# Two-stack sequence model on one core: the branch products of layers 1 and 2 as split products

## The chip, the cores and the metric

The kernel runs on one core of a Trainium2 chip. The time is that of the device for one execution, in microseconds (us). TensorE (PE in the profile) multiplies, VectorE (DVE), ScalarE (ACT) and GpSimd (POOL) work on elements, SyncE (SP) issues the weight loads.

## The reference

256 tokens of width 1024 pass through four layers, two of a first kind (called layers 1 and 2 here, `L` = 0 and 1 in the code) and two of a second. All is float32. A layer of the first kind has four mixers (retention, SSD, gated linear attention, mLSTM), each 256 wide, whose outputs are weighed with gates and merged:

```
    u = h @ w_in
    ...
    y_ret = (head_rmsnorm(o, ret_norm_g).reshape(bsz, seq, MIX_W) * jax.nn.silu(rg)).astype(h.dtype)
    ...
    ybr = jnp.stack([y_ret, y_ssd, y_gla, y_ml], axis=2)
    gates = jax.nn.sigmoid(mgate.reshape(bsz, seq, N_BRANCH, D_MODEL))
    merged = jnp.sum(gates * jnp.einsum('bsnv,nvd->bsnd', ybr, w_branch), axis=2)
    return merged @ w_out
```

The change is about the `einsum` with `w_branch`: four products of 256 tokens x 256 by 256 x 1024 in each of the two layers.

## The kernel before

The 256 tokens are two tiles (`T` = 2) of 128 rows. The branches are taken in the order SSD, mLSTM, retention, gated attention; `b` is 0 to 3 in this order, and "branch 0" to "branch 3" below are these.

**Two kinds of product.** Most products are split: the weights are cut into pieces of 1024 columns. ScalarE rounds a piece to a high part (`w_hi`, written by `high_parts`, line 1859), GpSimd or VectorE subtracts it from the original and has the low part (`w_lo`, lines 844 and 2926), and TensorE makes three matmuls of the rounded type for one exact product (`split_product`, lines 1004 to 1006: high x high, low rows x high weights, high rows x low weights). The four branch products of layers 1 and 2 (`merge` on TensorE, line 1130) are plain float32 matmuls, straight from the loaded weights in `ring`; the hardware runs each as two passes.

**Places.** There are four places for pieces (`NPIECE`). A piece's high part is written when the piece four before it has been used by TensorE. Pieces are made in one order for all engines; `M` is the number of the first piece of a layer behind its first six projections. Before the change M+8 to M+39 are the gates' 32 pieces, whose low parts GpSimd makes (two instructions of 512 columns for a piece), and M+40 on are those of the output product, by VectorE.

**Banks.** Four PSUM banks (`pb`) go round among the jobs listed in `bank_jobs1`. A job may open its bank when the job four before it has been emptied. The last jobs ahead of the gates of branch 2 are the four of product 0 (two halves `h` of 512 columns, two tiles `i`): the gates of branch 2 need the first two of these emptied, by VectorE. The gates of branch 3 need the second and third of product 1.

**The order.** Each engine runs a list written out by hand (the functions `mixers`). On TensorE the scans' small products stand between halves of the gates' jobs (`gate`). For each branch VectorE takes its output `y` from PSUM, norms it (`head_norm`, lines 2344 to 2355, with `rsqrt`, lines 2247 to 2254, for the root) and signals `y_ready`. TensorE turns it (`y_turned`, line 1119), ScalarE copies the turned rows to `yT` (line 1792), and TensorE makes the product (`merge`). VectorE weighs it with the gates and adds it up (`merge`, lines 2377 to 2385). On VectorE the head norm of branch `b + 1` stands ahead of the merge of branch `b`. The weights lie in two slots of `ring`, loaded alternately by SyncE when the slot's last reader is done.

## Time and profile before

| | us |
|---|---|
| median of three runs | 2436.46 (2432.53 to 2437.64) |
| profiled execution, its own time | 2435.75 |
| its span | 2433.9 |
| TensorE busy | 2353.2 (97%) |
| VectorE busy | 1693.3 (70%) |
| ScalarE busy | 1407.6 (58%) |
| GpSimd busy | 427.9 (18%) |
| the 128 plain passes of the branch products, first to last start | 177.9 to 733.1 |

The span is what the profiler sees from the first to the last instruction; the execution's own time is 1.85 us longer. A line number in a row is that of the listing. "x16" is the number of instructions in the row, and "[0.43 <-..]" behind a row is how long the engine stood idle before it and what ended that. Times of starts are from the span's start. A row of the timeline with several instructions gives the time from the first start to the last end.

### The profile page before, as it was taken

How to read it: one execution, taken by the hardware profiler on the slowest of the kernel's cores; microseconds unless marked ns; L12 is line 12 of the kernel's file. 1: busy time of each engine (PE TensorE's matmuls, PEld its weight loads, DVE VectorE, ACT ScalarE, POOL GpSimd, SP SyncE). 2: the span in 40 equal slices, each digit the busy share in tenths (PEclk: the TensorE clock that was granted, in tenths of full speed). 3: DMA queues.
4: the chain of work that ended last, by engine and by line, in shares of the span. 5: the costliest groups of instructions: out<-in, count | busy, mean ns of one | idle time of the engine just before them, and what ended most of it. 6: DMA issues, size and time to landing. Idle time of an engine off the chain costs nothing.

```text
span 2433.9 us, 32355 instructions
## 1 busy us (share of the span) xinstructions
PE 2353.2 (97%) x11899; PEld 1953.9 (80%) x11899; DVE 1693.3 (70%) x2327; ACT 1407.6 (58%) x1779; POOL 427.9 (18%) x381
## 2 busy tenths in 40 slices
PE   7999999899998999999999999899989989998998
PEld 7986788798867888888888888788878878887886
DVE  5847655576576999989889898883475557347555
ACT  4543344455433888888878888645444444645443
POOL 1256000004540000000000000075600007560000
PEclk9999999999998999999999999999999999999999
DMA  6534666244335999999999999844475634447450
GB/s 215 191 121 172 208 209 207 89 165 149 129 139 191 362 344 351 361 341 367 344 344 366 342 360 350 296 140 158 160 258 171 204 115 137 170 163 247 167 196 35
DMA packets 384550, 549.77 MB, mean 226 GB/s; under 512 B 27410, under 2 KB 283784, under 8 KB 384312
## 3 DMA queue, kind: packets, MB, share of 16 engines
q1 hardware_dynamic: 380080, 535.82, 64.9%
q0 software_dynamic: 4080, 11.96, 1.5%
q8 instruction: 69, 1.13, 0.2%
q10 hardware_dynamic: 288, 0.59, 0.1%
q14 instruction: 33, 0.27, 0.0%
HBM read 547.28 MB, written 1.05 MB: 225 GB/s over the span
## 4 chain that ended last, share of the span: by engine, by line
PE 85%; DVE 6%; DMA 4%; POOL 2%; issue 1%; ACT 1%; SPq 0%; ACTq 0%; DVEq 0%; POOLq 0%
PE mb L1004 14%; PE mb L1006 14%; PE mb L1005 14%; PE pb L1004 10%; PE pb L1006 9%; PE pb L1005 9%; DMA ring<-in_w_in 2%; PE pb L1130 2%; DVE w_lo L2926 2%; POOL w_lo L844 1%; PE mb L1396 1%; DMA down_w<-in_moe_w 1%; PE pb L1474 1%; DVE conv L2299 1%; PE mb L1157 1%
## 5 line engine op out<-in xcount | busy, mean ns | idle before, releaser
L2926 DVE TENSOR_TENSOR w_lo<-ring,w_hi 128x1024 fp32r<-128x1024 f32 x464 | 558.7, 1221 | 172.9 <-ACT w_hi L1859 126.3
L844 POOL TENSOR_TENSOR w_lo<-ring,w_hi 128x512 fp32r<-128x512 f32 x304 | 390.6, 1321 | 1324.1 <-DVE xn L2733 797.0
L1859 ACT ACTIVATE w_hi<-ring 128x1024 fp32r<-128x1024 f32 x360 | 371.4, 1055 | 272.5 <-PE pb L1006 163.0
L1004 PE MATMUL mb<-w_hi,hT_hi 128*128 128x512 f32 x1232 | 492.1, 399 | 1.6 <-DVE xg_lo L2926 1.1
L1006 PE MATMUL mb<-w_lo,hT_hi 128*128 128x512 f32 x1232 | 481.2, 391 | 0.0
L1004 PE MATMUL pb<-w_hi,hT_hi 128*128 128x512 f32 (+1 forms) x928 | 349.8, 377 | 5.2 <-POOL w_lo L844 3.2
L2926 DVE TENSOR_TENSOR w_lo<-down_w,w_hi 128x1024 fp32r<-128x1024 f32 x242 | 293.7, 1222 | 84.7 <-ACT w_hi L1859 79.3
L1006 PE MATMUL pb<-w_lo,hT_hi 128*128 128x512 f32 (+1 forms) x928 | 342.2, 369 | 0.0
L1005 PE MATMUL pb<-w_hi,low_rows 128*128 128x512 f32 (+1 forms) x928 | 341.9, 368 | 0.0
L2028 ACT ACTIVATE w_hi<-ring 128x1024 fp32r<-128x1024 f32 x256 | 268.5, 1057 | 30.4 <-PE mb L1006 21.9
L1005 PE MATMUL mb<-w_hi,xg_lo 128*128 128x512 f32 x704 | 274.6, 390 | 0.0
L1004 PEld LDWEIGHTS mb<-w_hi,hT_hi 128*128 128x128 f32 x1232 | 231.6, 188 | 49.8 <-DVE w_lo L2926 3.6
L1006 PEld LDWEIGHTS mb<-w_lo,hT_hi 128*128 128x128 f32 x1232 | 231.5, 188 | 49.6
L1004 PEld LDWEIGHTS pb<-w_hi,hT_hi 128*128 128x128 f32 x928 | 175.8, 189 | 39.4 <-DVE merged L2788 3.8
L1005 PE MATMUL mb<-w_hi,low_rows 128*128 128x512 f32 x528 | 206.0, 390 | 0.0
L2028 ACT ACTIVATE w_hi<-down_w 128x1024 fp32r<-128x1024 f32 x176 | 187.0, 1063 | 31.0 <-PE mb L1006 26.7
L1006 PEld LDWEIGHTS pb<-w_lo,hT_hi 128*128 128x128 f32 x928 | 175.7, 189 | 29.7
L1005 PEld LDWEIGHTS pb<-w_hi,low_rows 128*128 128x128 f32 x928 | 175.9, 190 | 27.1 <-issue 0.3
L2926 DVE TENSOR_TENSOR w_lo<-third_gu,w_hi 128x1024 fp32r<-128x1024 f32 x132 | 159.3, 1221 | 37.4 <-ACT w_hi L1859 30.6
L1005 PEld LDWEIGHTS mb<-w_hi,xg_lo 128*128 128x128 f32 x704 | 132.5, 188 | 24.8
L1004 PE MATMUL mb<-w_hi,fhT_hi 128*128 128x512 f32 x352 | 137.7, 391 | 0.0
L1006 PE MATMUL mb<-w_lo,fhT_hi 128*128 128x512 f32 x352 | 137.3, 390 | 0.0
(515 smaller groups left out, 3592.1 us busy)
## 6 DMA issues: line engine op xcount, KB each, us to landing
ring<-in_moe_w SPq DMA_DIRECT2D x128, 1024.0 KB, 9.5
ring<-in_w_in SPq DMA_DIRECT2D x50, 2048.0 KB, 8.0
down_w<-in_moe_w SPq DMA_DIRECT2D x88, 1024.0 KB, 12.3
third_gu<-in_moe_w SPq DMA_DIRECT2D x48, 1024.0 KB, 11.0
down_w<-in_w_ffn_down SPq DMA_DIRECT2D x22, 1024.0 KB, 10.0
ring<-in_w_out SPq DMA_DIRECT2D x8, 2048.0 KB, 7.9
ring<-in_ffn_w SPq DMA_DIRECT2D x16, 1024.0 KB, 8.0
ring<-in_w_ffn_gate SPq DMA_DIRECT2D x16, 1024.0 KB, 5.4
```

The costliest lines, as they stand in the source:

```text
L844: ins = nc.gpsimd.tensor_tensor(w_lo[:, m % NPIECE, cols], source[m][0][:, cols], w_hi[:, m % NPIECE, cols].bitcast(F32), ALU.subtract)
L1004: mm(o, a_hi, hi, start=start, stop=False)
L1005: mm(o, a_lo, hi, start=False, stop=False)
L1006: return mm(o, a_hi, lo, start=False, stop=stop)
L1130: ins = mm(bank[:], yT[:, b % 2, kk, i * P:(i + 1) * P], w[:, kk, h * 512:(h + 1) * 512], start=kk == 0, stop=kk == 1)
L1157: ins = mm(banks[i][:, h * w:(h + 1) * w], probs[:, h, at:at + P], v(j, h), start=n == 0, stop=n == len(parts) - 1)
L1396: ins = mm(mb[2 + half][:, (k % 4) * P:(k % 4 + 1) * P], xn[:, i, k * P:(k + 1) * P], sel[:, i], start=i == 0, stop=i == T - 1)
L1474: ins = mm(bank[:, 0:n], hT[:, k, i * P:(i + 1) * P], wv[:, k], start=k == 0, stop=k == KD - 1)
L1859: f(w_hi[:, m % NPIECE], src, ACT.Copy).then_inc(w_hi_ready, 1)
L2028: f(w_hi[:, n % NPIECE], expert_piece(c, q), ACT.Copy).then_inc(e_hi_ready, 1)
L2299: ins = stt(out=conv[:, blk, s:S], in0=ch_in[:, blk, 0:S - s], scalar=w(3 - s), in1=conv[:, blk, s:S], op0=ALU.mult, op1=ALU.add)
L2926: return tt(dst, src, hi.bitcast(F32), ALU.subtract)
```

## The change

The branch products of layers 1 and 2 become split products, by the function that layers 3 and 4 already used (`merge2`, now `merge`). Their weights become pieces, two for each branch, that stand between those of the gates: behind M+23 come two of product 0, then eight of gates 2, two of product 1, four of gates 3, two of product 2, four of gates 3, two of product 3; the output product begins at M+48. GpSimd makes their low parts. The turned rows are written as a high part by ScalarE (`turned_high`, to `y_odd_hi`) and a low part by VectorE (`turned_low`, to `y_rows_lo`). Each branch's weights have a slot of `ring` for themselves, in two loads; the slot is free when the low parts are made.

```diff
-    items = [("proj", c) for c in range(len(CHUNKS1))]
-    items += [("gate", b, h) for b in range(NBR) for h in range(2)]
+    items = [("proj", c) for c in range(len(CHUNKS1))] + [("gate", b, h) for b in range(2) for h in range(2)]
+    merge = lambda b: [("merge", b, h) for h in range(2)]
+    items += merge(0) + [("gate", 2, 0), ("gate", 2, 1)] + merge(1) + [("gate", 3, 0)] + merge(2) + [("gate", 3, 1)] + merge(3)
...
-                low_parts(MIX[L] + HEAD_PIECES + 8, MIX[L] + HEAD_PIECES + 40)
+                low_parts(MIX[L] + HEAD_PIECES + 8, MIX[L] + HEAD_PIECES + 48)
...
+            def merge_rows(L, b, hs=range(2)):
+                pe.wait_ge(dve_emptied, BK[L].emptied(("yturn", b))[1])
+                merge(L, b, row_parts, hs)
+
+            def merge(L, b, parts, hs=range(2)):
+
+                n_k = branch_k(L, b)
                 for h in hs:
...
+                    banks = [open_bank(BK[L], ("merge", b, h, i)) for i in range(T)]
+                    for q in range(n_k // 2):
+                        m = PC.of[(L, "merge", b, h, q)]
+                        hi, lo = parts[q]
+                        pe.wait_ge(*low_done(m))
+                        for i in range(T):
+                            it = slice(i * P, (i + 1) * P)
+                            for kk in range(2):
+                                k = 2 * q + kk
+                                ins = split_product(banks[i][:], hi[:, kk, it], lo[:, kk, it], m, slice(kk * 512, (kk + 1) * 512),
+                                                    k == 0, k == n_k - 1)
...
-                high_to(M + 24)
-                yturned(L, 0)
+                row_high = row_parts[0][0]
+                turned_high(L, ("yturn", 0), row_high)
+                high_to(M + 26)
                 gate(L, 1, 1)
-                high_to(M + 28)
+                high_to(M + 30)
                 act.wait_ge(gla_arg, 2 * L + 1)
...
                 v.wait_ge(o_read, 4 * L + 2)
+                turned_low(L, 1, ("yturn", 0), row_parts[0])
                 head_norm(L, 1, 3, u_ml[:, :, ML_O:ML_O + MW], False)
                 merge(L, 0)
...
                 v.wait_ge(o_read, 4 * L + 3)
+                turned_low(L, 2, ("yturn", 1), row_parts[0])
                 head_norm(L, 2, 0, u_ret[:, :, 768:1024], False)
                 merge(L, 1)
...
                 head_norm(L, 3, 2, u_gla[:, :, 4 + MW:], False)
-                low_range(M + 40, M + 42)
-                merge(L, 3)
+                turned_low(L, 4, ("yturn", 3), row_parts[0])
+                merge(L, 3, (0,))
+                low_range(M + 48, M + 50)
+                merge(L, 3, (1,))
```

ScalarE, layer 1, from the copies of retention's turned rows (`conv`) to the first exponents of the gated attention, before:

```order
L1953 ACTIVATE conv<-mb 128x512 x2
L1792 ACTIVATE yT<-pb 128x512
L1792 ACTIVATE gates<-pb 128x512 x2
L1859 ACTIVATE w_hi<-ring 128x1024 x4
L1960 ACT_TABLE_LOAD
```

and now:

```order
L1961 ACTIVATE conv<-mb 128x512 x2
L1896 ACTIVATE y_odd_hi<-pb 128x512
L1865 ACTIVATE w_hi<-ring 128x1024 x2
L1798 ACTIVATE gates<-pb 128x512 x2
L1865 ACTIVATE w_hi<-ring 128x1024 x4
L1969 ACT_TABLE_LOAD
```

Two high parts, those of product 0, now stand behind the turned rows and ahead of the second half of the gates of branch 1.

VectorE, layer 1, at the head norm of branch 1, now (before, the same without the row of `y_rows_lo`):

```order
L2569 TENSOR_TENSOR y<-mb,small 128x256 x2
L2934 TENSOR_TENSOR y_rows_lo<-pb,y_odd_hi 128x512
L2347 TENSOR_TENSOR scratch<-y 128x512
L2349 TENSOR_REDUCE small<-scratch 128x8
L2350 TENSOR_SCALAR small<-small 128x8
L2250 TENSOR_SCALAR small<-small 128x8
L2251 TENSOR_TENSOR small<-small 128x8
```

It goes on with the root's other six small instructions, three of 512 columns on `y`, and the merge of product 0. The turned rows' low part has come ahead of the norm.

VectorE, the end of the mixers of layer 1, before:

```order
L2355 TENSOR_TENSOR y<-y,u_gla 128x512
L2926 TENSOR_TENSOR w_lo<-ring,w_hi 128x1024 x2
L2382 TENSOR_TENSOR gates<-pb,gates 128x512
L2385 TENSOR_TENSOR merged<-merged,gates 128x512
L2382 TENSOR_TENSOR gates<-pb,gates 128x512
```

and now:

```order
L2358 TENSOR_TENSOR y<-y,u_gla 128x512
L2934 TENSOR_TENSOR y_rows_lo<-pb,y_odd_hi 128x512
L2393 TENSOR_TENSOR gates<-pb,gates 128x512
L2396 TENSOR_TENSOR merged<-merged,gates 128x512
L2393 TENSOR_TENSOR gates<-pb,gates 128x512
L2396 TENSOR_TENSOR merged<-merged,gates 128x512
L2934 TENSOR_TENSOR w_lo<-ring,w_hi 128x1024 x2
L2393 TENSOR_TENSOR gates<-pb,gates 128x512
```

The two pieces of the output product have moved from ahead of the merge of product 3 to between its halves. GpSimd has in each of the two layers, in one row each, now

```order
L858 TENSOR_TENSOR w_lo<-ring,w_hi 128x512 x80
```

where 64 of the same kind (line 844) stood.

## Rows read from the trace of the kernel before

**Rows 1.** The page: busy time of TensorE; the chain's shares by engine.
```profile
PE 2353.2 (97%) x11899; PEld 1953.9 (80%) x11899; DVE 1693.3 (70%) x2327; ACT 1407.6 (58%) x1779; POOL 427.9 (18%) x381
...
PE 85%; DVE 6%; DMA 4%; POOL 2%; issue 1%; ACT 1%; SPq 0%; ACTq 0%; DVEq 0%; POOLq 0%
```

**Rows 2.** Timeline of TensorE, layer 1: start, duration, instruction.
```profile
177.24 0.39 PE L1004 MATMUL pb<-w_hi,hT_hi 128*128 128x512 f32 x1
...
177.92 7.03 PE L1130 MATMUL pb<-ring,yT 128*128 128x512 f32 x16
184.88 0.70 PE L1146 MATMUL mb<-conv 64*128 64x256 f32 x4
...
186.39 0.50 PE L1004 MATMUL pb<-w_hi,hT_hi 128*128 128x512 f32 x1
...
219.57 0.50 PE L1004 MATMUL pb<-w_hi,hT_hi 128*128 128x512 f32 x1
```

**Rows 3.** All of line 1130: ns least/median/most, first and last start.
```profile
L1130 PE MATMUL pb<-ring,yT x128: 590/592/697, 177.9 to 733.1; 128*128 128x512 f32 x128
```

**Rows 4.** Timeline of GpSimd, layer 1, and one row of layer 2 (647.83).
```profile
179.74 10.00 POOL L844 TENSOR_TENSOR w_lo<-ring,w_hi 128x512 fp32r<-128x512 f32 x8 [9.68 <-ACT w_hi L1859]
194.98 10.37 POOL L844 TENSOR_TENSOR w_lo<-ring,w_hi 128x512 fp32r<-128x512 f32 x8 [5.24 <-ACT w_hi L1859]
215.25 10.01 POOL L844 TENSOR_TENSOR w_lo<-ring,w_hi 128x512 fp32r<-128x512 f32 x8 [9.90 <-ACT w_hi L1859]
...
647.83 9.96 POOL L844 TENSOR_TENSOR w_lo<-ring,w_hi 128x512 fp32r<-128x512 f32 x8 [9.72 <-ACT w_hi L1859]
```

**Rows 5.** Timeline of ScalarE, layer 1.
```profile
173.16 0.61 ACT L1792 ACTIVATE yT<-pb 128x512 f32<-128x512 f32 x1
176.76 0.60 ACT L1792 ACTIVATE gates<-pb 128x512 f32<-128x512 f32 x1 [2.99 <-PE pb L1006]
...
178.62 3.88 ACT L1859 ACTIVATE w_hi<-ring 128x1024 fp32r<-128x1024 f32 x4
```

**Rows 6.** Timeline of VectorE, layer 1, head norm of branch 1 to merge 0.
```profile
174.55 0.69 DVE L2344 TENSOR_TENSOR scratch<-y 128x512 f32<-128x512 f32 x1
...
179.27 0.69 DVE L2355 TENSOR_TENSOR y<-y,u_ml 128x512 f32<-128x512 f32 x1
180.00 0.69 DVE L2377 TENSOR_TENSOR merged<-pb,gates 128x512 f32<-128x512 f32 x1
```

**Rows 7.** VectorE beside GpSimd: head norm 0 (layer 1), and layer 4.
```profile
149.35 1.66 DVE L2344 TENSOR_TENSOR scratch<-y 128x512 f32<-128x512 f32 x1
...
2047.88 0.16 DVE L2251 SCALAR_TENSOR_TENSOR small<-small 128x2 f32<-128x2 f32 x1
2048.02 5.07 POOL L844 TENSOR_TENSOR w_lo<-ring,w_hi 128x512 fp32r<-128x512 f32 x4 [3.58 <-ACT w_hi L1859]
2048.08 1.26 DVE L2252 TENSOR_TENSOR small<-small 128x2 f32<-128x2 f32 x1
2049.37 1.22 DVE L2253 TENSOR_TENSOR small<-small 128x2 f32<-128x2 f32 x1
```

**Rows 8.** VectorE, layer 1: last exponents; end of head norm 2.
```profile
202.82 1.37 DVE L2404 TENSOR_TENSOR ch_in<-gT 128x128 f32<-128x128 f32 x1
...
213.15 0.69 DVE L2355 TENSOR_TENSOR y<-y,u_ret 128x512 f32<-128x512 f32 x1
```

**Rows 9.** End of the mixers of layer 1: VectorE, and TensorE's next product.
```profile
260.96 0.69 DVE L2382 TENSOR_TENSOR gates<-pb,gates 128x512 f32<-128x512 f32 x1 [5.58 <-PE pb L1130]
...
267.48 1.28 DVE L2926 TENSOR_TENSOR low_rows<-pb,hT_hi 128x512 fp32r<-128x512 f32 x2
...
269.01 0.47 PE L1004 MATMUL pb<-w_hi,hT_hi 128*128 128x512 f32 x1 [0.25 <-DVE low_rows L2926]
```

**Rows 10.** Stretches of 4 us: busy time by engine, granted clock (PEclk), DMA.
```profile
1580.00:1584.00 4.00, 2.74 (x10) 2.10 (x11) 2.33 (x2) 2.50 (x5) 0.00 (x0) 0.50 0.68 250
1584.00:1588.00 4.00, 4.00 (x9) 2.07 (x8) 2.61 (x10) 3.76 (x6) 0.00 (x0) 0.67 0.01 2
```

150 lines of the change are left out of this document (65 added, 85 removed).

## The prediction

> **What bounds the kernel now.** I read the shares of busy time first, then the chain that ended last, then the timeline of each engine in layer 1 from 170 to 270 us. TensorE is busy for 97% of the span and carries 85% of the chain [rows 1]: a stage gets shorter only if TensorE has less to do in it, and longer as soon as TensorE stands still. In the mixers of layers 1 and 2 it hardly does. The branch products cost, by the first of them, 184.88 - 177.92 = 6.96 us for 16 passes of 0.43 us [rows 2]; 128 such passes are in the whole trace [rows 3], so eight products. A split product has three matmuls, and from one such group to the next thing on the engine it is 177.92 - 177.24 = 0.68 us, 0.227 us a matmul [rows 2].
>
> Beside TensorE three engines matter. GpSimd makes the low parts of the gates' weights: four pieces (8 halves) take 10.0 us, 1.25 a half, and between two such groups it sits idle for 9 to 10 us [rows 4]. ScalarE makes the high part that GpSimd waits for. VectorE norms each branch's rows (the head norm) and then empties that branch's product banks. The reader is to see how these fall: GpSimd starts at 179.74 us, and the head norm of branch 1 runs from 174.55 to 179.96 [rows 4, 6]. In that norm the eleven instructions with two inputs in SBUF have GpSimd idle beside them.
>
> **What the change saves on TensorE.** Each product becomes 24 split matmuls: 24 x 0.227 = 5.44 us instead of 6.96, so -1.52 us, and eight times that is -12.2 us. Two of the four in a layer give it in full, if nothing else stands in the way. For the product of branch 2, whose halves stand between the rounds of the third scan, the next round waits for VectorE's copies, which do not get shorter: between 0 and -1.5 us, and I take -0.4, as VectorE's work between the halves is unchanged. For branch 3 see the end of the layer.
>
> **What it adds.** ScalarE: eight more high parts a layer at 0.97 us (3.88 for four [rows 5]); at the first place it has the time, being idle from 173.77 to 176.76, and nothing queued behind is late. GpSimd: eight more pieces of 2.5 us a layer; TensorE needs 12 x 0.227 = 2.72 us for a piece, so GpSimd keeps up in number. VectorE: four low parts of turned rows a layer, 0.64 to 0.69 us each by the same subtraction out of PSUM (two in 1.28 [rows 9]). Weight loads are the same bytes. The second load of gate weights behind a branch's slot no longer waits for that product's end; it is hidden now and stays so.
>
> **Where it hurts, place 1.** The order of ScalarE's work puts the two pieces of the branch product ahead of the gates of branch 1, right behind the turned rows. Turned rows 173.16 to 173.77, high parts to 174.7 and 175.7: GpSimd starts at 174.8 and not at 179.74. From there it has six pieces in a row, two of the product and four of the next gates, 12 x 1.25 = 15 us. VectorE now begins the head norm at 174.55 + 0.69 = 175.2, in the middle of it.
>
> What then happens can be seen in layer 4, in the same root. With GpSimd idle a subtraction of 2 columns with two SBUF inputs takes 0.16 us; once GpSimd's four halves begin at 2048.02, the same kind takes 1.26 and 1.22 us, one for each half of GpSimd [rows 7]. A large one (512 columns) took 1.66 instead of 0.69 us [rows 6, 7]. The reduction and the scalar instructions, with one input, keep their time. So the head norm, 5.45 us before, gets:
> - seven small ones (root) at a pitch of 1.28 instead of 0.20: +7.6 us
> - four large ones, 0.7 for the first and 0.9 for each of the rest: +3.4 us
> - the low part of the turned rows ahead of it: +0.7 us
>
> Together +11.7 us, so VectorE comes to the first product bank at 191.7 instead of 180.0 and has emptied two at 193.2. GpSimd is slowed by some 1.5 us and still works at 191, so the cover lasts for the whole norm. TensorE is through with product 0 at 183.4 and with the retention scores at 185.0, and the next gate job needs those two banks: it starts at 193.4 where it started at 186.39 [rows 2]. **+7.0 us**, as a standstill of some 8.4 us.
>
> The Trainium skill has this as a rule (SBUF — State Buffer, Who interferes with whom): a VectorE instruction with two SBUF inputs and a GpSimd instruction that reads SBUF exclude one another for the whole instruction. By that rule the forecast is as above, and the trace agrees (1.26 us against 0.16).
>
> **The clock.** After a standstill of 6.32 us in layer 3 the granted clock was 0.50 in the next 4 us and 0.67 in the 4 after [rows 10]: half speed (1.2 GHz) for 2.7 + 2.6 = 5.4 us, a loss of 2.7 us of work. A standstill of 8 us should bring the same.
>
> **Place 2.** The same meeting comes again at branch 2. Before, its norm ran in a pause of GpSimd (it ends at 213.84; GpSimd starts at 215.25, having paused 9.90 us [rows 4, 8]). Now pieces of product 1 are made in that pause, again right behind the turned rows. TensorE needs the third of product 1's banks for the gates of branch 3, at 219.57 before [rows 2]. Two ends. From below, if VectorE's second norm costs TensorE nothing: 7.0 + 2.7 (clock) - 1.5 (product 1) = +8.2 us. From above: VectorE is 8.9 us late behind product 0; the exponents that follow are already slowed now (1.37 us each [rows 8]) and stay as they are, and the norm gets 8 us longer: +17 us. I take +12.5, the middle: GpSimd works on two pieces and then pauses for a load, so part of the small instructions pass at 0.2 us.
>
> **The end of the layer.** Here nothing stands between the turning of branch 3's rows and its product. High part 0.6 us (as now), then VectorE's low part 0.7: TensorE starts 0.7 us later, and its product is 1.5 shorter. But VectorE, which sat idle for 5.58 us and had made two pieces of the output product beforehand [rows 9], now makes them (2.4 us) between the two halves of the merge. First bank filled 0.35 us later than before, four tiles of 1.45 and the pieces 2.4 in a row: the merge ends at 269.5 instead of 267.6, and the output product starts at 270.9 instead of 269.01 [rows 9]: **+1.9 us**, between +0.5 (if the pieces fit while a bank is awaited) and +2.4. The third norm meets GpSimd too, but has 4.5 us to spare: 0 to +1.5, taken as 0.
>
> **Sum.** Per layer 12.5 - 0.4 + 1.9 = 14.0 us. GpSimd's starts in layer 2 lie 468.1 us after those of layer 1 [rows 4], the same program: twice, +28.0. Against the profiled execution's own 2435.75 us (span 2433.9 and 1.9 around it; 0.7 below the median 2436.46 of the three runs): 2463.8, said as 2464. With the ends: (8.2 - 0.4 + 1.9) x 2 = +19 gives 2455; (17 - 0.4 + 1.9) x 2 = +37 gives 2473.
>
> **Rivals.**
> - The exclusion misses the norms. It decides at one point: if GpSimd takes up the product's pieces only when the norm is done (5 us later than I think), or if VectorE gets in ahead of each half. Then products 0 and 1 give 3.0, product 2 gives 0.4, the end costs 1.9: -1.5 a layer, 2432.7: not slower, and within 0.2% of before. Against it: ScalarE's idle time from 173.77, and rows 7. Chance 0.12.
> - The exclusion holds only in part, each small instruction losing half of what I say: place 1: two banks emptied at 180.0 + 5.9 + 1.5 = 187.4, +1.0 us; place 2 at half of the norm's 8, +4, in place of the 12.5; no clock loss. 4 - 0.4 + 1.9 = 5.5 a layer, 2447. For it: the small ones pass quickly whenever GpSimd waits. Chance 0.10.
> - More: the upper end of place 2, a second fall of the clock there (2.7) and the third norm late (1.5): 22.7 a layer, 2481. Chance 0.15.
> - That the change does not do what it says: the order of instructions shows the split product, GpSimd's 80 halves instead of 64, and VectorE's four low parts, so 0.03 for something unseen.
>
> **Numbers.** Forecast 2464, chance 0.60, its own range 2455 to 2474. The range of 8 in 10 reaches from 2447 into the partial case to 2482 in the heavy one. About 0.2% (4.9 us) is what a measurement here tells from no change. Faster by over that only in the upper part of the first rival and the unseen: 0.04; same 0.09; slower 0.87.
>
> **What will show it.** Right: the small instructions of branch 1's head norm at 1.2 us, GpSimd busy from 175 on, TensorE waiting for VectorE ahead of gates 2 by some 8 us and again ahead of gates 3, a granted clock of half behind each, and the output product starting some 14 us later in layer 1. Split matmuls of the products at 0.227 us. Wrong: a head norm of 6 us, or a VectorE that waits for TensorE at product 0; then the first rival holds. If place 1 is as said and place 2 is not, the time is near 2455.

## The result

| | median us | runs | ratio to before, 95% interval |
|---|---|---|---|
| before | 2437.05 | 4 (2432.53 to 2438.03) | |
| after | 2486.33 | 4 (2477.51 to 2488.58) | 1.0198 (1.0181 to 1.0216) |

The change costs 49 us; 2464 with a range of 2447 to 2482 was forecast, so the time lies 22 us above the forecast and 4 above the range. The direction held, and so did the mechanism at place 1; the size did not, and two terms of the sum were wrong in more than size. The profiled execution of after took 2488.6 us, its span is 2486.8.

The rows say first where the 49 us are. These are TensorE's waits in the whole trace of after: what waited, for whom, us in total, how often, the longest. Before has none of them but the one for `merged` ahead of line 960 (974 now), which was 2.0 in total there.

```profile
PE pb L1018 <- DVE merged L2388: 16.5, 2, 8.3
PE pb L1018 <- DVE merged L2391: 15.1, 2, 8.1
...
PE pb L974 <- DVE merged L2396: 6.7, 2, 3.3
...
PE pb L1018 <- DVE y_rows_lo L2934: 3.4, 2, 1.9
```

The first row is place 1 (gates of branch 2), the second place 2 (gates of branch 3), the other two the end of the layer.

**Place 1.** GpSimd, then VectorE, then TensorE, in the timeline of layer 1 (start, duration, instruction), against [rows 2, 4, 6]:

```profile
176.48 15.81 POOL L858 TENSOR_TENSOR w_lo<-ring,w_hi 128x512 fp32r<-128x512 f32 x12 [4.72 <-ACT w_hi L1865]
```

```profile
176.85 1.47 DVE L2347 TENSOR_TENSOR scratch<-y 128x512 f32<-128x512 f32 x1
...
179.55 1.22 DVE L2250 TENSOR_SCALAR small<-small 128x8 int32<-128x8 int32 x1
180.80 1.22 DVE L2251 TENSOR_TENSOR small<-small 128x8 f32<-128x8 f32 x1
...
192.87 0.69 DVE L2358 TENSOR_TENSOR y<-y,u_ml 128x512 f32<-128x512 f32 x1
193.60 2.87 DVE L2388 TENSOR_TENSOR merged<-pb,gates 128x512 f32<-128x512 f32 x4
```

```profile
195.11 0.77 PE L1018 MATMUL pb<-w_hi,hT_hi 128*128 128x512 f32 x1 [8.26 <-DVE merged L2388]
```

The turned rows of branch 0 came 1.7 us later in this execution than in that of before (between 40 and 60 us the granted clock was 0.83 on average, in before 0.91). Without that, VectorE is at the product's banks at 191.9 (191.7 forecast) and TensorE restarts at 193.4 (193.4 forecast).

**Place 2.** In the second norm three of the eight small instructions of the root are held, five pass in 0.17 us while GpSimd waits for a high part, and all four large ones are held. The gates of branch 3 start 14.8 us later than before [rows 2], again without the 1.7. First the row of before at which VectorE takes the output of branch 2, then after:

```profile
207.66 0.74 DVE L2577 COPY y<-mb 128x256 f32<-128x256 f32 x2
```

```profile
217.64 0.74 DVE L2589 COPY y<-mb 128x256 f32<-128x256 f32 x2
...
221.74 1.21 DVE L2250 TENSOR_SCALAR small<-small 128x8 int32<-128x8 int32 x1
...
225.25 1.22 DVE L2257 SCALAR_TENSOR_TENSOR small<-small 128x8 f32<-128x8 f32 x1
...
231.63 0.70 DVE L2390 TENSOR_TENSOR pb<-pb,gates 128x512 f32<-128x512 f32 x1
...
236.06 0.77 PE L1018 MATMUL pb<-w_hi,hT_hi 128*128 128x512 f32 x1 [7.00 <-DVE merged L2391]
```

The 14.8 are three parts. VectorE takes the output of branch 2 8.3 us later (217.64 - 173.68 against 207.66 - 171.99, counted from the turning of branch 0's rows). From there to the merge it takes 14.0 us where it took 6.2 (213.88 in before), 7.8 more. And from the merge to the gates of branch 3 it is 4.4 us (236.06 - 231.63) where it was 5.7 (219.57 - 213.88), 1.3 less: before, TensorE's own work came last there.

**The clock.** Stretches of 4 us of after; the columns are the busy time of TensorE, its weight loads, VectorE, ScalarE and GpSimd, then the granted clock, the share of DMA and GB/s. Before has 1.00 at all of these places.

```profile
192.00:196.00 4.00, 0.89 (x2) 0.82 (x3) 3.83 (x6) 0.00 (x0) 0.29 (x1) 0.50 0.61 171
...
236.00:240.00 4.00, 3.94 (x9) 3.14 (x10) 3.90 (x4) 0.00 (x0) 0.40 (x1) 0.50 0.60 185
264.00:268.00 4.00, 4.00 (x16) 3.42 (x16) 3.40 (x9) 0.00 (x0) 0.00 (x0) 0.57 0.90 320
288.00:292.00 4.00, 2.53 (x10) 2.43 (x11) 3.18 (x5) 1.15 (x2) 0.00 (x0) 0.56 0.00 0
```

So there are four falls to 1.2 GHz in this layer, and I had counted the first. The third comes between the rounds of the third scan, behind idle times of 1.46 us (ahead of 260.71) and 0.88 us (ahead of 262.09) and small matmuls, the fourth at the output product.

**One measure for all runs.** The four executions of after lie up to 11 us apart, and the code outside the changed part, the same in all kernels, took between 2203 and 2216 us in their traces. The trace has a cleaner mark, though it is that of one execution: from the first turning of branch 0's rows to the last turning of `merged`, in each of the two layers. In after it is 173.7 to 291.0 and 665.1 to 785.1.

```profile
L974 PE MATMUL pb<-cst,merged x16: 270/347/446, 285.1 to 291.0; 128*128 128x128 f32 x16
```

| kernel | this stretch in layers 1, 2 (us) | over before, both | median us | ratio to before |
|---|---|---|---|---|
| before | 96.5, 96.5 | | 2434 to 2437 | |
| after | 117.3, 120.0 | +44.3 | 2486.33 | 1.0198 (1.0181 to 1.0216) |

The two profiled executions differ by 52.9 us in their spans, the medians by 49.3. 44.3 of the 52.9 lie in these stretches, for which the forecast was 28. Of the other 8.6, 1.7 lie ahead of the first stretch. 1.9 lie right behind the two stretches (to the first turning of line 986 it takes 18.5 and 17.3 us, in before 17.0 and 16.9), where the clock of the fourth fall is still half (0.59 from 292 to 296 us). The last 5.0 lie in code that is the same in both.

The same marks split the 44.3 by stage; the forecast's terms are beside them, for one layer.

| from, to | before, layers 1, 2 | after, layers 1, 2 | more, layers 1, 2 | forecast |
|---|---|---|---|---|
| turning of branch 0 to gates of branch 3 (places 1 and 2) | 47.58, 47.58 | 62.38, 63.55 | 14.8, 16.0 | 12.5 |
| to the turning of branch 2 (clock behind place 2) | 5.58, 5.57 | 7.72, 7.26 | 2.1, 1.7 | 0 |
| to the turning of branch 3 (rounds of the third scan, product 2) | 32.37, 32.01 | 33.60, 35.25 | 1.2, 3.2 | -0.4 |
| to the last turning of `merged` (end of the layer) | 11.0, 11.4 | 13.6, 14.0 | 2.6, 2.6 | 1.9 |

### The profile page after: what moved, and what is told of

It reads as the page before. It is cut to its first block, busy times and chain, and to the rows that moved or that the text cites. A ratio compares the mean times of both kernels' runs of the same rounds, so it can differ in the third digit from the quotient of the medians.

```text
span 2486.8 us, 32577 instructions
## 1 busy us (share of the span) xinstructions
PE 2367.9 (95%) x11963; PEld 1984.4 (80%) x11963; DVE 1725.6 (69%) x2335; ACT 1423.6 (57%) x1795; POOL 475.9 (19%) x413
## 4 chain that ended last, share of the span: by engine, by line
PE 84%; DVE 9%; DMA 2%; ACT 2%; issue 1%; SPq 1%; POOL 0%; ACTq 0%; DVEq 0%
PE mb L1018 14%; PE mb L1020 14%; PE mb L1019 14%; PE pb L1018 10%; PE pb L1020 10%; PE pb L1019 10%; DMA down_w<-in_moe_w 2%; DVE w_lo L2934 1%; PE pb L1500 1%; PE mb L1422 1%; DMA ring<-in_w_in 1%; PE pb L1088 1%; PE pb L1089 1%; PE pb L1090 1%; PE mb L1453 1%
## 5 line engine op out<-in xcount | busy, mean ns | idle before, releaser
L858 POOL TENSOR_TENSOR w_lo<-ring,w_hi 128x512 fp32r<-128x512 f32 x336 | 438.6, 1343 | 1354.8 <-DVE xn L2749 799.2
L1865 ACT ACTIVATE w_hi<-ring 128x1024 fp32r<-128x1024 f32 x376 | 389.1, 1056 | 287.5 <-PE pb L1020 188.9
L1018 PE MATMUL pb<-w_hi,hT_hi 128*128 128x512 f32 (+1 forms) x928 | 357.5, 385 | 36.7 <-DVE merged L2388 16.5
L1019 PE MATMUL pb<-w_hi,low_rows 128*128 128x512 f32 (+1 forms) x928 | 348.0, 375 | 0.0
L1020 PE MATMUL pb<-w_lo,hT_hi 128*128 128x512 f32 (+1 forms) x928 | 347.8, 375 | 0.0
L2038 ACT ACTIVATE w_hi<-ring 128x1024 fp32r<-128x1024 f32 x256 | 268.3, 1057 | 33.4 <-PE mb L1020 22.2
L1018 PEld LDWEIGHTS pb<-w_hi,hT_hi 128*128 128x128 f32 x928 | 180.4, 194 | 72.1 <-DVE merged L2388 16.9
```

Source lines behind the costliest of these rows:

```text
L858: ins = nc.gpsimd.tensor_tensor(w_lo[:, m % NPIECE, cols], source[m][0][:, cols], w_hi[:, m % NPIECE, cols].bitcast(F32), ALU.subtract)
L1018: mm(o, a_hi, hi, start=start, stop=False)
L1019: mm(o, a_lo, hi, start=False, stop=False)
L1020: return mm(o, a_hi, lo, start=False, stop=stop)
L1865: f(w_hi[:, m % NPIECE], src, ACT.Copy).then_inc(w_hi_ready, 1)
L2038: f(w_hi[:, n % NPIECE], expert_piece(c, q), ACT.Copy).then_inc(e_hi_ready, 1)
```

## Experiments

All start from the kernel after, where nothing else is said.

### Is it the exclusion, and does it go by GpSimd's instruction?

**Quarters.** GpSimd makes each low part in four instructions of 256 columns.

```diff
-                    for half in range(2):
-                        cols = slice(half * PIECE // 2, (half + 1) * PIECE // 2)
+                    for half in range(4):
+                        cols = slice(half * PIECE // 4, (half + 1) * PIECE // 4)
```

> GpSimd makes each low part in four instructions of 256 columns and not in two of 512; nothing else changes. Theory (exclusion): a VectorE instruction that needs the shared way into SBUF waits for the end of the GpSimd instruction under way, so the wait goes with the size of that instruction: the small instructions of head norm 1 (layer 1) fall from 1.22 us to about 0.65, the norm from 16.7 us (176.85 to 193.56) to about 12, TensorE's wait ahead of the gates of branch 2 from 8.3 us to 3 or 4, and the kernel from 2486 to about 2465. Rival (rate: both engines merely share a bandwidth): the small ones keep 1.2 us, the norm its 16.7 us, and the time stays at 2486 or grows by GpSimd's extra instructions.

Measured 2468.17 us (2462.41 to 2488.06), ratio 1.0157 (1.0106 to 1.0207); the stretch 105.9 and 107.1. A small instruction now takes what a quarter takes:

```profile
177.65 0.65 DVE L2251 TENSOR_TENSOR small<-small 128x8 f32<-128x8 f32 x1
```

Half the work of GpSimd's instruction, half the time of VectorE's (1.22 to 0.65), and the total of GpSimd is not less (18.59 us for what took 15.81). VectorE's time here is a wait for one instruction of GpSimd, not a lower rate.

**No root.** In norms 1 and 2 the root is left out and the mean of squares taken as the factor (the values are then not normed).

```diff
-                rsqrt(rr, ss)
+                if b in (1, 2):
+                    link(ts(rr, ss, 1.0, None, ALU.mult))
+                else:
+                    rsqrt(rr, ss)
```

> The root in the head norms of branches 1 and 2 is left out (eight small instructions with a scalar or two inputs, one short copy in their place); the values of these branches are not normed, all else runs. Theory: in head norm 1 each of them costs a whole GpSimd instruction, so seven fewer make it 8.7 us shorter (16.7 to 8.0), the first wait for banks falls from 8.3 us to nearly 0, and the second, whose norm lost some 3.5 us to them, from 7 to 2 or less; the time falls by 25 to 35 us to 2451 to 2461. Rival (added work: VectorE has got more to do and that is what TensorE waits for): seven instructions of 0.2 us, 1.4 us shorter, four times in the kernel: 2480.

Measured 2464.85 us in one run, 4 us above the upper end expected; stretch 107.2 and 107.2. The wait ahead of gates 2 is gone (0.7 us left), that ahead of gates 3 is 5.4. So the roots carry more than half of the loss, and not all of it.

### Can the meeting be avoided by order? Two misses

**High parts early.** ScalarE makes the products' high parts ahead of the turned rows, so that GpSimd has done product 0 before the norm.

```diff
-                high_to(M + 24)
+                high_to(M + 26)
                 act.wait_ge(qkt_mm, L + 1)
...
-                high_to(M + 34)
+                high_to(M + 35)
...
+                high_to(M + 36)
                 turned_high(L, ("yturn", 1), row_high)
-                high_to(M + 36)
```

> Only ScalarE's order changes: the two high parts of product 0 are made before the copies of retention's turned rows, and those of product 1 one before and one behind the second exponential, ahead of the turned rows. So GpSimd works on product 0's pieces right behind those of gates 1, in its pause, and is done when head norm 1 begins. The work of every engine is the same. Theory: head norm 1 takes 5.5 to 7 us in place of 16.7, head norm 2 some 8 in place of 12.6; TensorE no longer waits for banks ahead of gates 2 (8.3 us) and gates 3 (7.0), nor runs at half clock behind either: 18 to 22 us a layer back, and the kernel at 2440 to 2447, the rest being the end of the layer. Rival (added work on VectorE, or both banks opened at once): waits stay, 2486.

Measured 2480.16 us, ratio 1.0196 (1.0169 to 1.0223), stretch 115.6 and 119.2: nothing gained that is clear of noise. Place 1 did what was expected (standstill 2.8 instead of 8.3 us), and place 2 took nearly all of it back:

```profile
PE pb L1018 <- DVE merged L2391: 19.8, 2, 10.4
```

**Merge first.** VectorE empties product 0 and makes the retention weights ahead of head norm 1.

```diff
-                head_norm(L, 1, 3, u_ml[:, :, ML_O:ML_O + MW], False)
                 merge(L, 0)
...
                 ins.then_inc(probs_ready, 1)
+                head_norm(L, 1, 3, u_ml[:, :, ML_O:ML_O + MW], False)
```

> Only VectorE's order changes at place 1: the merge of product 0 and the retention scores times the decay stand ahead of head norm 1, not behind it. The norm meets GpSimd as before. Theory: the norm stays long (GpSimd is busy until 191 or so, it begins at 188: some 8 us), but what is queued behind it is no longer the emptying of banks: no wait ahead of gates 2; the gates' half clock there goes; the wait ahead of gates 3 stays or shrinks by little, since VectorE's chain from there is as long: 6 to 10 us a layer back, 2466 to 2474. Rival (both engines slow each other everywhere, no queue effect): the wait ahead of gates 2 stays.

Measured 2487.06 us, ratio 1.0212 (1.0192 to 1.0232), stretch 122.0 and 122.9. No standstill at place 1 at all, and 12.1 us at place 2. Two different ways of clearing place 1 gave nothing, so my picture of two costs side by side (7.0 and then some) was wrong. The end of place 2 is set by VectorE's own chain, and what TensorE wins ahead of it goes to GpSimd: the places for pieces come free earlier, and GpSimd works through VectorE's exponents and its second norm. In layer 1 of this run seven of the last eight exponents took 1.24 to 1.38 us, in after three.

### Take the operands out of GpSimd's way

The low part of the turned rows reads one operand from PSUM, and took 0.69 us in the middle of four halves of GpSimd, about half of the 1.28 that two such take in [rows 9]. In after:

```profile
246.04 5.06 POOL L858 TENSOR_TENSOR w_lo<-ring,w_hi 128x512 fp32r<-128x512 f32 x4 [9.64 <-ACT w_hi L1865]
```

```profile
248.37 0.69 DVE L2934 TENSOR_TENSOR y_rows_lo<-pb,y_odd_hi 128x512 fp32r<-128x512 f32 x1
```

So a bank might do what no order did. Added lines shift the numbers in these kernels: 2411 to 2414 there are 2388 to 2391 of after, 2440 and 2441 are the exponents, 2459 and 2465 are 2433 and 2439 of after.

**Roots through PSUM.** In norms 1 and 2, the root's small operands stand in columns 384 to 407 of a bank that is free then; each instruction reads one from there. The formula is written so that none needs two from PSUM: r*r*m becomes (r*m)*r, and there is one instruction more. TensorE may write the bank after the first large product.

```diff
+                link(ts(sb.bitcast(I32), m.bitcast(I32), -0.5, ROOT_SEED, ALU.mult, ALU.add))
+                link(tt(t, sb, m, ALU.mult))
+                link(tt(t, t, sb, ALU.mult))
...
+                if b in (1, 2):
+                    ss, rr, tmp = mb[0][:, 384:392], mb[0][:, 392:400], mb[0][:, 400:408]
```

> The kernel after, but in the head norms of branches 1 and 2 the small operands of the root stand in a free PSUM bank, so that each small instruction reads one operand from PSUM and at most one from SBUF (one more instruction for that, nine instead of eight), and the first large product reads the factors from PSUM too. TensorE may write that bank only after that product. GpSimd and ScalarE are unchanged. In the kernel after, such a mixed instruction already stands beside GpSimd (low part of the turned rows, 0.69 us), and the all-SBUF ones cost 1.2 us each. Exclusion theory (only two operands in SBUF, or none elsewhere, wait for GpSimd): small instructions at 0.17 to 0.2 us, the first large product near 0.7, each of the two norms some 8 us shorter, the standstills ahead of the gates of branches 2 and 3 down from 8.3 and 8.1 us to under 2 each, the clock falls behind them gone: some 14 to 17 us a layer, 2452 us (2448 to 2460). Rival, that VectorE is slowed by GpSimd whatever memory it reads: small instructions at 1.2 us, no change, 2486. Rival from the run with product 0 merged first, that the time won at place 1 is given back at place 2: 2470 to 2480, with the second standstill still over 5 us.

Measured 2456.73 us (2452.24 to 2464.4), ratio 1.0099 (1.0073 to 1.0124), stretch 104.9 and 108.6. GpSimd and VectorE at the same time:

```profile
172.13 16.52 POOL L858 TENSOR_TENSOR w_lo<-ring,w_hi 128x512 fp32r<-128x512 f32 x12 [4.74 <-ACT w_hi L1865]
```

```profile
174.95 0.17 DVE L2266 TENSOR_SCALAR small<-mb 128x8 int32<-128x8 int32 x1
175.15 0.17 DVE L2267 TENSOR_TENSOR mb<-small,mb 128x8 f32<-128x8 f32 x1
...
178.24 1.67 DVE L2381 TENSOR_TENSOR y<-y,u_ml 128x512 f32<-128x512 f32 x1
```

The mixed instructions take 0.17 us under twelve halves of GpSimd; the large one whose two operands are in SBUF takes 1.67, as such ones do in after (1.71 at 189.46). So what held the small ones was their operands in SBUF. One row does not fit: the large instruction just ahead (177.52, line 2380), with both operands in SBUF too, took 0.69 us, and no run shows why it passed. The Trainium skill's rule (SBUF — State Buffer, Who interferes with whom), quoted in the prediction for two SBUF inputs, agrees with the other rows. The same section also counts `tensor_scalar`, which has one input, among the operations that can contend with GpSimd, and `tensor_reduce` not. The traces agree: the first instruction of the root (line 2250), a `tensor_scalar` with a single input, took 1.22 us at 179.55 in after, and the reduction kept its 0.69. The prediction took both as free, rightly only for the reduction.

**And the exponents.** The exponents of the third scan subtract SBUF from SBUF. The gate sums are copied once to a free bank.

```diff
+                else:
+                    v.wait_ge(probs_ready, 3 * L + 3)
+                    link(cp(mb[3][:, 0:S], gT[:]))
...
-                    ref = g[:, :, 0, b - 1:b].to_
+                    ref = mb[3][:, 0:S].rearrange("p (m s b) -> p m s b", s=2, b=b)[:, :, 0, b - 1:b].to_
```

First alone, with the roots left in SBUF:

> The kernel after with only the exponents' operand in PSUM; the roots stay in SBUF. It prices the exponents' part. In the trace of after four or five of the sixteen exponents took 1.27 to 1.37 us and VectorE then waited 4.0 us for ScalarE's exponentials. Theory: the exponents are covered as long as the standstill at place 1 holds TensorE and ScalarE back: 0 to 1.5 us a layer, 2485 us (2482 to 2487); the exponents only count once the roots are fast. Rival, that exponents and roots add up: 2478 or less.

Measured 2482.14 us, ratio 1.0188 (1.0173 to 1.0204), stretch 115.9 and 119.0: 2.4 us of 44.3, since both standstills stay. Then with the roots:

> Roots and exponents with one operand in PSUM, the end of the layer as the change has it. With e13 it prices the end of the layer when nothing stands still before it, with e8 the exponents when the roots are fast. Theory: the end costs what e5_tail gave back, 4 to 5 us a layer: 2446 us (2443 to 2449). Rival, that the end is smaller without the clock falls ahead of it: 2441 or less.

Measured 2446.02 us, ratio 1.0046 (1.0031 to 1.006), stretch 100.2 and 100.2. So the exponents are worth 13.1 us in the stretches once the roots are fast and 2.4 before. How many GpSimd holds goes with where they fall: in layer 1, eight of the sixteen in before, three in after, ten with the roots through PSUM.

### The end of the layer

VectorE makes the output product's two low pieces around the turned rows' low part and merges branch 3 in one go; ScalarE makes the second piece's high part sooner.

```diff
-                high_to(M + 48)
+                high_to(M + 49)
...
-                turned_low(L, 4, ("yturn", 3), row_parts[0])
-                merge(L, 3, (0,))
-                low_range(M + 48, M + 50)
-                merge(L, 3, (1,))
+                low_range(M + 48, M + 49)
+                turned_low(L, 4, ("yturn", 3), row_parts[0])
+                low_range(M + 49, M + 50)
+                merge(L, 3)
```

> The kernel after, with the end of the layer done in another order: VectorE makes the first low piece of the output product ahead of the low part of the last turned rows and the second right behind it, and merges branch 3 in one go; ScalarE makes the second piece's high part ahead of the second half of the last gates. Places 1 and 2 are untouched. Theory: the merge of branch 3 ends 2.4 us earlier and the clock fall at the output product goes: 2.3 to 4.2 us a layer, 2479 us (2476 to 2483). Rival: the low part of the turned rows comes later by the pieces' time and TensorE's product with it: 2484 to 2488.

Measured 2476.87 us (2471.13 to 2480.39), ratio 1.018 (1.0163 to 1.0197), stretch 113.9 and 115.5 (3.4 and 4.5 less). The wait of 3.3 us is 1.1 and the clock behind it stays whole:

```profile
PE pb L974 <- DVE merged L2396: 2.1, 2, 1.1
```

```profile
288.00:292.00 4.00, 4.00 (x19) 3.33 (x18) 1.91 (x3) 1.87 (x2) 0.00 (x0) 1.00 0.62 189
```

### What the clock costs

Extra matmuls into a bank that nobody reads fill the standstills: 32 at place 1 and 36, then 56, at place 2.

```diff
                 pe.wait_ge(o_read, 4 * L + 2)
+                for n in range(32):
+                    mm(mb[0][:], hT_hi[:, 0, 0:P], hT_hi[:, 0:2].rearrange("p k s -> p (k s)"), start=True, stop=True)
```

> The kernel after, with extra matmuls of 512 columns into a bank that nobody reads: 32 ahead of the retention scores and 36 ahead of the first round of the third scan, some 7.3 and 8.2 us of TensorE's work in the two standstills of 8.3 and 8.1 us. Nothing of the computation changes. It prices the clock falls behind the standstills apart from the standstills. Theory: the granted clock stays near 1.0 behind both; the first fall costs nothing by itself, since the second standstill ends by VectorE's chain whenever TensorE gets there, so only the second (2.1 us a layer) comes back: 2482 us (2479 to 2485). Rival: both falls count (2.7 + 2.1 a layer): 2476. Rival: the clock falls anyhow, or the extra work delays TensorE: 2486 or above.

> The run e9_busy with 56 instead of 36 extra matmuls at the second place, as the first 36 ended 4 us before the standstill did and the clock still fell (0.84, 0.50, 0.81 in three stretches of 4 us). In e9_busy the time won by the full clock behind place 1 was given back: GpSimd got its high parts sooner, worked 16 us in a row beside the exponents and the second norm, and the gates of branch 3 started at the same time. Theory: now the second fall goes too and 2 us a layer come back: 2482 us (2479 to 2485). Rival: no change, 2487.

Measured 2486.98 (ratio 1.0218, 1.0201 to 1.0235) and 2486.26 us (1.0208, 1.0191 to 1.0226). The stretches are 124.8 and 121.6, then 120.1 and 122.6, longer than in after though the times are not. In the first only the fall at place 1 goes (at place 2 the clock is 0.84, 0.50 and 0.81 from 232 to 244 us). In the second the clock is whole from 184 to 260 us:

```profile
236.00:240.00 4.00, 4.00 (x42) 3.32 (x39) 3.86 (x5) 0.00 (x0) 0.00 (x0) 1.00 0.23 84
...
264.00:268.00 4.00, 4.00 (x16) 3.50 (x16) 2.10 (x4) 0.00 (x0) 0.00 (x0) 0.54 1.05 402
```

Both falls are gone and nothing is won; both expectations (2482) missed. From branch 0's turned rows to the gates of branch 3 it takes 62.4 us in after (236.06 - 173.7), 66.0 with the first fall filled and 66.4 here (236.70 - 170.3), where TensorE comes to the gates about 0.5 us behind VectorE's third bank. GpSimd got its high parts sooner: it works 16.3 us in a row over the second norm, all eight of the root's small instructions are held (three in after) and seven of the last eight exponents (three). Behind the gates of branch 3 the whole clock gives back 1.2 us in layer 1 and 0.2 in layer 2, since the third fall, between the scan's rounds, covers two stretches (0.61 and 0.54) where after has one. The first fall of the clock, which I had priced at 2.7 us, had no price of its own as long as VectorE set the next start.

### All together, and one more surprise

> All that helps, together: the root's operands in PSUM in norms 1 and 2, the product pieces' high parts ahead of the turned rows (as in e3), and the end of the layer in the order of the run e5_tail. Theory: both standstills and their clock falls gone and the end at the cost of before, 2440 us (2435 to 2447): what is left against before are the slowed large instructions of the norms and VectorE's added low parts. It decides whether split branch products can beat the kernel before at all: their own gain is 2.7 to 3.4 us a layer. Rival, that the gain is given back at the next place where VectorE is late (the locked exponents, the third norm): 2455 or more.

This has the roots through PSUM, the early high parts and the new end. Measured 2454.47 us, ratio 1.0089 (1.0067 to 1.0112), stretch 105.7 and 105.8, not the 2440 expected. The early high parts were again the suspect, so the next pair has the exponents too, and differs in them alone:

> The run e10_psum_early_tail, and besides the exponents of the third scan take one of their two operands from PSUM (the gate sums copied once into a free bank, 0.42 us). In e10 ten of the sixteen exponents of a layer took 1.21 to 1.38 us instead of 0.28, and the second head norm began at 211.0 us with TensorE waiting 3.1 us for the turned rows' low part behind it and 3.1 us for the merge. Theory (what is left of place 2 is the exponents' waiting for GpSimd): exponents at 0.28 us, y copied some 8 to 10 us earlier, both 3.1 us standstills and their clock falls gone: 7 to 10 us a layer, 2438 us (2434 to 2444). Rival, that the second norm's start hangs on ScalarE's exponentials or on TensorE's values: exponents at 0.28 us, but 2448 or more.

> The run e12_psum_exponents with the product pieces' high parts back in the change's place, behind the turned rows. Whether GpSimd meets the norms is then left as the change has it, and only what VectorE reads is different. Theory: with one operand in PSUM the meeting costs only the large instructions of the norms, so this is within 3 us of e12. Rival, that the early high parts carry the gain: 5 us or more slower than e12.

With the early high parts 2452.24 us (1.006, 1.0042 to 1.0079; stretch 108.4 and 103.8), with the change's own order **2437.32** (1.0012, 1.0002 to 1.0023; 98.6 and 97.1). Both expectations missed: the first was 2438, the second was to be within 3 us of the first, and the early order costs 15 us. Why, stands in ScalarE's timeline, early order first, then the change's:

```profile
200.66 1.06 ACT L1865 ACTIVATE w_hi<-ring 128x1024 fp32r<-128x1024 f32 x1 [2.55 <-PE pb L1020]
201.74 1.28 ACT L1974 ACT_TABLE_LOAD   x1
203.04 1.06 ACT L1974 ACTIVATE ch_in<-ch_in 128x1024 f32<-128x1024 f32 x1
```

```profile
197.06 1.28 ACT L1974 ACT_TABLE_LOAD   x1
198.35 1.06 ACT L1974 ACTIVATE ch_in<-ch_in 128x1024 f32<-128x1024 f32 x1
```

The piece of product 1, moved ahead of the second exponentials, waits there for its place, and the exponentials that VectorE needs stand behind it: 4.7 us later. VectorE takes the output of branch 2 at 209.83 instead of 203.27. The same edit was in "High parts early", so its miss had this cause too beside the exponents (in layer 1 there, all eight of the second half took 1.25 to 1.38 us).

In the better of the two, VectorE's exponents pass freely while GpSimd works (189.80 to 195.99), and TensorE waits 0.9 us ahead of the gates of branch 3 where it waited 7.0:

```profile
192.60 0.28 DVE L2441 TENSOR_TENSOR ch_in<-gT,mb 128x128 f32<-128x128 f32 x1
...
203.27 0.74 DVE L2614 COPY y<-mb 128x256 f32<-128x256 f32 x2
```

```profile
215.58 0.47 PE L1018 MATMUL pb<-w_hi,hT_hi 128*128 128x512 f32 x1 [0.89 <-DVE merged L2414]
```

### Which products are worth splitting

**Only branches 2 and 3**, the others in full passes as before, with the new end; operands stay in SBUF.

```diff
             gate_items(0); gate_items(1)
-            branch_items(L, 0, a["w_branch"][L, BR_ORDER[0]])
+            branch_item(0)
             gate_items(2)
-            branch_items(L, 1, a["w_branch"][L, BR_ORDER[1]])
+            branch_item(1)
```

> Half of the change: the products of branches 2 and 3 are split, those of branches 0 and 1 stay as before (full passes, unsplit rows, no pieces for GpSimd), with the end of the layer in the order of the run e5_tail. The head norms 1 and 2 then have GpSimd beside them as before. Theory: no standstill ahead of the gates of branches 2 and 3; the halves of product 2 save 0 to 1.5 us, the product of branch 3 saves 1.5 and pays 0.7 for the low part and what the pieces cost at the end: 2434 us, between 2431 and 2439, the same as before. Rival, that the products between the scan's rounds or the end of the layer carry a cost of their own (clock falls at 264 and 288 us in the trace of after): 2441 or more.

Measured 2440.5 us, ratio 1.0016 (1.0005 to 1.0026), stretch 97.3 and 99.0. No standstill at the gates, which start as in before (47.6 us behind the first turning); a fall of the clock at 244 to 248 us (0.60) remains. That is 1.5 us above the upper end expected (2439): no gain, a loss of 0.05 to 0.26%. From the turning of branch 2 to that of branch 3 it takes 33.60 and 35.27 us, as in after, where before has 32.37 and 32.01: split, product 2 costs 1.2 and 3.3 us with nothing late ahead of it.

**Only branches 0, 1 and 3**, with both PSUM edits and the new end. Product 2, between the scan's rounds, is again in full passes, with its rows unsplit and no pieces of it for GpSimd.

```diff
-                        merge_rows(L, 2, (rnd - 2,))
+                        merge_full(L, 2, (rnd - 2,))
```

> The run e13_psum_exp_late with the product of branch 2 back in full passes (unsplit rows, two pieces fewer for GpSimd, one low part fewer for VectorE); products 0, 1 and 3 stay split. In e13 the granted clock fell between the rounds of the third scan (0.91, 0.50, 0.50, 0.81 in four stretches of 4 us from 236 us), where the kernel before kept 1.00: there the shorter product leaves TensorE with more waiting for VectorE's copies. Theory: that fall goes, product 2 costs 0 to 1.5 us more by itself, products 0, 1 and 3 save 1.5 us each less 0.9 and 1.1 us of waits: 2 to 3 us a layer better than e13, 2432 us (2429 to 2436). Rival, that the fall comes in any case once the layer has small standstills: 2437 or more.

Measured **2432.70 us** (2427.95 to 2433.32, 12 runs) beside 2435.82 of before (24 runs): ratio 0.9983 (0.9974 to 0.9992). It is faster than both kernels, by 0.08 to 0.26% against before. The stretch is 93.9 and 95.5. The clock between the rounds, with product 2 split (first fence) and in full passes (second):

```profile
240.00:244.00 4.00, 4.00 (x21) 4.00 (x20) 2.19 (x4) 0.00 (x0) 1.13 (x1) 0.50 0.38 113
244.00:248.00 4.00, 4.00 (x12) 3.32 (x12) 2.85 (x9) 0.00 (x0) 0.00 (x0) 0.50 1.04 400
```

```profile
240.00:244.00 4.00, 4.00 (x31) 3.69 (x30) 3.73 (x7) 0.00 (x0) 1.23 (x2) 1.00 0.98 333
244.00:248.00 4.00, 4.00 (x19) 3.34 (x18) 3.62 (x12) 1.06 (x1) 1.49 (x2) 1.00 1.04 398
```

And TensorE's rows at the same place, split, then in full passes:

```profile
238.05 0.50 PE L1295 MATMUL mb<-conv,xs 32*128 32x128 f32 x8 [1.47 <-DVE probs L2465]
239.43 5.38 PE L1183 MATMUL mb<-u_gla,probs 128*128 128x64 f32 x24 [0.88 <-DVE probs L2459]
```

```profile
238.19 0.50 PE L1306 MATMUL mb<-conv,xs 32*128 32x128 f32 x8
239.57 2.89 PE L1194 MATMUL mb<-u_gla,probs 128*128 128x64 f32 x24 [0.88 <-DVE probs L2474]
```

The last round starts at the same time in both, when VectorE's copies are there (238.05 and 238.19). The full passes fill the time until then. Split, they leave TensorE idle for 1.47 us more, the clock falls, and the same 24 matmuls behind it take 5.38 us instead of 2.89. That is layer 1. In layer 2 of the kernel with full passes the clock fell there too, less (0.89 and 0.68 in two stretches; 0.79, 0.50 and 0.86 in three with product 2 split), without the 1.47 us ahead of it; from turning to turning it has 33.7 us where before has 32.0.

**The control:** the kernel before with the PSUM operands alone.

> The kernel before with only the PSUM operands (roots of head norms 1 and 2, exponents of the third scan), nothing split. In its trace VectorE is not late in this stretch: no wait of TensorE for it ahead of the gates of branches 2 and 3. Theory: no change, 2435 us (2432 to 2437), so what e13 has gained over the kernel after is the change's own cost removed and no gift that before would have had too. Rival, that the kernel before also hides a loss there: 2431 or less.

Measured 2435.32 us, ratio 0.9994 (0.9983 to 1.0006), stretch 97.0 and 96.2: no change, as expected. The PSUM operands are worth nothing without the change; they take back what it costs.

## Why the forecast was right in direction and wrong in size

Three terms of the sum failed. Place 2 was mis-sized (12.5 forecast, 14.8 and 16.0 measured in the two layers), product 2 was taken as a gain (-0.4) and is a cost (1.2 and 3.2), and the fall of the clock behind place 2 was put at nothing in the sum (2.1 and 1.7). The points below say why.

The stretches also give accounts by experiment, in us for both layers together:

| step | kernels compared | us |
|---|---|---|
| roots held by GpSimd | after, roots through PSUM | 44.3 - 20.5 = 23.8 |
| exponents held by GpSimd | roots; roots and exponents | 20.5 - 7.4 = 13.1 |
| end of the layer | that; with the new end | 7.4 - 2.7 = 4.7 |
| product 2 split | that; product 2 in full passes | 2.7 + 3.6 = 6.3 |
| what is left: products 0, 1, 3 split, less small waits | last kernel, before | -3.6 |

Sum 44.3. The edits were put in one after the other, so each figure is that of its place in this order; the exponents alone were 2.4, the new end alone 7.9. The stretch ends at the last turning of `merged` and so leaves out the half clock right behind it: with the old end there are 3.0 us more to the first turning of line 986 for both layers, with the new end none (roots and exponents in PSUM in both), so the end is 7.7 of the 8.7 us between these medians.

Point by point:

- **Split matmuls at 0.227 us, product 0 at 5.44 us.** Right: the first starts at 179.63 in after, the retention scores behind the last at 185.28, with 0.2 us of start-up.
- **Place 1: +7.0, standstill 8.4.** Right to 0.1 us (21.43 - 14.40 from the turning of branch 0 to the gates of branch 2), small instructions at 1.22 as said. The rule that decided it was confirmed by quarters and by PSUM operands. That it came out to a tenth is in part luck: eight small instructions of the root were held and not seven, and line 2350 a little, but of the four large ones the last was not (0.69 us at 192.87, as GpSimd had ended at 192.29).
- **Place 2: +12.5 in total, between 8.2 and 17.** This is the first term that failed: 14.8 and 16.0 measured, within its bounds but 2.3 and 3.5 above the middle. The middle had no row behind it. The upper end had the right sum: VectorE 8.9 us late and the norm 8 longer, measured 8.3 and 7.8, less 1.3. Five small instructions did pass quickly, as the middle had it, but the four large ones and three small ones were held all the same. The prediction also held that the exponents "are already slowed now and stay as they are". For the kernel after that did no harm: fewer were held than before, and freeing them gave 2.4 us. It failed as a picture: with the roots fast they are the second largest part (13.1 us for both layers), and part of why clearing place 1 gave nothing back. The places are one chain, whose end VectorE sets.
- **The clock: one fall of 2.7 in the sum.** Failed in count: four falls in layer 1, of which the rival "heavy" had two. And failed in kind: the fall behind place 1 cost nothing by itself, as the filled standstills showed, while those between the scan's rounds and at the output product did. Behind place 2 the half clock is 2.1 us in the trace of after (from the gates of branch 3 to the turning 7.72 instead of 5.58 us; 1.7 in layer 2), for which the sum had nothing; filled, it gave back only 1.2 and 0.2, as the next fall was longer.
- **Product 2: -0.4 a layer, between 0 and -1.5.** Failed, and on the wrong side: +1.2 and +3.2 in after, 1.2 and 3.3 with only two products split, 3.2 a layer (6.3 / 2) as the last edit prices it. I looked for what the copies would let through and not for what TensorE does meanwhile. The range ended at 0 for the case in which nothing is won; a cost was not in it. This is the largest single miss beside place 2.
- **End of the layer: +1.9, between 0.5 and 2.4.** The mechanism was right: from turned rows to the output product 13.7 to 14.0 us in after where it was 11.5, so +2.2 to +2.5, the upper end. The clock fall behind it was missing (1.5 and 0.4 us beyond the last turning in after); new order and whole clock gave back 3.4 and 4.5 alone and 2.4 a layer after the other edits.
- **Third norm: 0.** No wait for it was seen at that place.
- **Sum.** For both layers forecast 28, measured 44.3. By the stages of after: the places 25 against 30.8, +5.8; the clock behind place 2, +3.8; product 2, 4.5 against -0.8, +5.3; the end 5.3 against 3.8, +1.5. Together the 16.3 that lack, within rounding. What lies outside the stretches was not in the sum; 1.7 us of it are at the start of the program, where the clock differs from one execution to the next (0.83 in after's profile, 0.91 in before's, 1.00 in most later ones).

The rival "exclusion misses the norms" (2432.7) is refuted by the small instructions at 1.22 us; that the kernel with product 2 in full passes reaches its number (2432.70) is a coincidence, as it saves by other terms. "In part" (2447) falls with the eight of eight held at place 1. "Heavy" (2481) was nearest.

What stays open: why the clock falls between the rounds. With product 2 split it fell in each trace looked at, in both layers, behind the idle time of 1.47 us. Without that idle time it stayed whole in both layers of before and in layer 1 with full passes, and fell in layer 2 there. More than this the runs do not show. The 5.0 us behind the half clock, in code that is the same in both kernels, have no cause shown. The extra matmuls and "Merge first" made the stretches longer (by 5 to 9 us for both layers) and not the time, so a few us of any single trace are not explained.

## What to carry over

When work for GpSimd is put beside VectorE, list every VectorE instruction in the window that touches SBUF only, small ones above all: each can cost one whole GpSimd instruction (reductions did not). Give one operand of each a place in PSUM, or split GpSimd's instruction, before changing the order; clearing one wait of a chain moves the loss to the next.

A matmul that is hidden behind a wait need not be made shorter: here it kept TensorE busy, and with it, in layer 1, the clock. Shorten those on the path, leave those under cover.

## What the runs showed of the hardware

- With one operand in PSUM an instruction of VectorE on 8 columns takes 0.17 us under a running GpSimd instruction, with its operands in SBUF 1.22 beside GpSimd's halves (12 in 15.81 us, 1.32 each) and 0.65 beside quarters (24 in 18.59 us, 0.77 each). A large one is held too (1.67 against 0.69), though not each time (0.69 at 177.52 with the roots through PSUM).
- An instruction with a single SBUF input was held as well (line 2250, 1.22 us at 179.55 in after; line 2350, 0.43 instead of 0.17). The reduction kept its 0.69 us.
- Copying 256 columns to PSUM takes 0.43 us, and pays for sixteen exponents.
- Behind a standstill of 3.3 us the granted clock was 0.56 and 0.59 in the two stretches of 4 us from 288 us on in after, and behind idle times of 1.46 and 0.88 us with matmuls of 128 columns between them 0.57. With the 0.88 alone it stayed at 1.00 in both layers of before and in layer 1 with product 2 in full passes, and fell to 0.89 and 0.68 in layer 2 there.
